# The down biases' sums in the ninth expert pair, samples' totals in four parts, ring slots at multiples of 512 bytes

## The reference, cut to what matters

```
hx = layer_norm(DN_ALPHA * x_all + o_cat @ w_out, ln1_g, ln1_b)
logits = hx @ w_router + b_router
top_val, top_idx = lax.top_k(logits, 4)                  # of 32 experts
comb = sum(one_hot(top_idx, 32) * softmax(top_val))      # 288 x 32, four non-zero a row
for e in range(32):
    gu = hx @ w_gate_up[e] + b_gate_up[e]                # 1024 x 2048
    act = clipped SwiGLU(gu)
    f += comb[:, e] * (act @ w_down[e] + b_down[e])      # 1024 x 1024
y = layer_norm(DN_ALPHA * hx + f, ln2_g, ln2_b)
```

## Time and profile before

| | |
|---|---|
| median of 3 runs | 1166.18 us (1163.85 to 1167.03) |
| the profiled execution's own time | 1164.79 us |
| its span | 1162.8 us |
| TensorE (PE) matmuls busy | 1105.6 us, 95% (5478 matmuls, 5479 weight loads) |
| VectorE (DVE) / ScalarE (ACT) / GpSimd (POOL) busy | 293.7 / 203.9 / 30.0 us |
| moved by DMA | 454.23 MB, mean 391 GB/s |
| granted TensorE clock | 0.995 of full speed |

### The profile page before, as it was taken

The page is one execution under the profiler, slowest core; times in us unless marked ns, Lnnn a source line. Parts: engine busy times, 40 slices in busy tenths (PEclk is TensorE's granted clock), DMA queues, the critical chain, the costliest instruction groups (busy, mean ns, idle before and its releaser), DMA issues.

```text
span 1162.8 us, 14168 instructions
## 1 busy us (share of the span) xinstructions
PE 1105.6 (95%) x5478; PEld 467.7 (40%) x5479; DVE 293.7 (25%) x734; ACT 203.9 (18%) x481; POOL 30.0 (3%) x65
## 2 busy tenths in 40 slices
PE   7999998999999999999999999999999999999996
PEld 5876764433333333333333333333333333333331
DVE  1453756720303021212121212020202030303123
ACT  1332422411111110202020101010101011111111
POOL 0110111000000000000000000000000000000001
PEclk9999999999999999999999999999999999999998
DMA  9958879799999999999999999999999999999992
GB/s 341 348 184 274 284 259 388 293 380 422 424 429 427 428 428 427 429 427 429 427 429 428 429 427 429 428 429 428 430 427 430 427 430 427 430 428 425 405 411 79
DMA packets 62843, 454.23 MB, mean 391 GB/s; under 512 B 6563, under 2 KB 19507, under 8 KB 35540
## 3 DMA queue, kind: packets, MB, share of 16 engines
q1 hardware_dynamic: 60322, 440.97, 91.7%
q0 software_dynamic: 1728, 10.75, 2.5%
q10 hardware_dynamic: 754, 1.98, 0.5%
HBM read 450.14 MB, written 11.93 MB: 397 GB/s over the span
## 4 chain that ended last, share of the span: by engine, by line
PE 69%; DMA 25%; DVE 2%; ACT 2%; SPq 2%; issue 1%
DMA ring<-in_w_gate_up 24%; PE bank L1167 18%; PE bank L1118 18%; PE bank L676 5%; PE bank L995 5%; PE bank L699 5%; PE bank L1272 2%; PE bank L702 2%; PE bank L860 2%; PE bank L1194 2%; PE bank L991 1%; PE bank L1302 1%; PE bank L817 1%; ACT xtok L1382 1%; ACT actT L1382 1%
## 5 line engine op out<-in xcount | busy, mean ns | idle before, releaser
L1118 PE MATMUL bank<-ring,xg 128*64 128x512 f32 x1904 | 419.3, 594 | 25.7 <-DMA ring<-in_w_gate_up 25.7
L1118 PEld LDWEIGHTS bank<-ring,xg 128*64 128x64 f32 x1904 | 141.3, 137 | 295.3 <-issue 295.2
L1167 PE MATMUL bank<-ring,actT 128*64 128x512 f32 x960 | 216.1, 597 | 3.9 <-ACT actT L1382 3.9
L2038 DVE TENSOR_TENSOR acc<-acc,bank 128x512 f32<-128x512 f32 x60 | 41.3, 688 | 496.8 <-PE bank L1194 496.7
L1532 ACT ACTIVATE sig<-gate 128x256 f32<-128x256 f32 x64 | 26.7, 417 | 541.8 <-DVE gate L2020 541.8
L1167 PEld LDWEIGHTS bank<-ring,actT 128*64 128x64 f32 x960 | 66.7, 137 | 120.3 <-issue 114.5
L2020 DVE TENSOR_SCALAR gate<-bank 128x256 f32<-128x256 f32 x64 | 26.8, 419 | 196.7 <-PE bank L1118 177.8
L699 PE MATMUL bank<-xT,wblk 128*128 128x288 f32 x256 | 67.1, 417 | 2.1 <-DMA wblk<-in_w_in 2.1
L1522 ACT ACTIVATE xg<-bank,small 128x128 f32<-128x128 f32 x128 | 48.0, 457 | 96.7 <-PE bank L676 96.7
L995 PE MATMUL bank<-hx,pick 128*128 128x512 f32 x128 | 59.2, 605 | 0.0
L1194 PE MATMUL bank<-ybuf,spread 128*128 128x512 f32 x120 | 58.4, 618 | 0.0
(11 more groups left out here) (256 smaller groups left out, 728.3 us busy)
## 6 DMA issues: line engine op xcount, KB each, us to landing
ring<-in_w_gate_up SPq DMA_DIRECT2D x119, 2048.0 KB, 25.2
ring<-in_w_down SPq DMA_DIRECT2D x63, 2048.0 KB, 26.8
ring<-in_w_gate_up SPq DMA_DIRECT2D x16, 1024.0 KB, 19.2
wblk<-in_w_in SPq DMA_DIRECT2D x12, 1024.0 KB, 8.3
kring<-in_cache_k_moba SPq DMA_DIRECT2D x16, 256.0 KB, 5.8
vring<-in_cache_v_moba SPq DMA_DIRECT2D x16, 256.0 KB, 5.6
out<-in_state_k_win POOLq DMA_DIRECT2D x8, 512.0 KB, 4.3
out<-in_state_v_win POOLq DMA_DIRECT2D x8, 512.0 KB, 5.6
```

What stands on the lines that cost most here:

```text
L1118: ins = nc.tensor.matmul(bank[n][64 * e:64 * e + 64, :], xg[:, k, 64 * e:64 * e + 64], w[e][:, 512 * n:512 * n + 512], start=False, stop=( ...
L1167: ins = nc.tensor.matmul(bank[4 + half][64 * e:64 * e + 64, :], actT[:, j, 64 * e:64 * e + 64], w[e][:, at:at + 512], start=(j == 0), stop ...
L2038: V.tensor_tensor(o, o, new, ALU.add).then_inc(S.added, 1)
```

## The change

The three parts are these. First, the work with the down biases moves from pair 14 to pair 8 on TensorE, ScalarE and VectorE; for this the loops over pairs 2 to 13 are cut in two, with pairs 8 and 9 written out between them on TensorE (pair 8 on the other two). Second, VectorE writes the samples' part, ALPHA * gain * hx, straight into `acc_s` in four instructions of 32 x 256, where it wrote `samp_x` in two of 32 x 512 and zero to `acc_s`; TensorE's four products with `ident`, VectorE's second addition and the tile `samp_x` go. Third, the ring begins at a multiple of 512 bytes (87552, up from 87168). `first` keeps its address: both expressions give 62464.

```
-    first = place("first", [128, 4096], at=cursor[0] - 16384)
+    first = place("first", [128, 4096], at=share_at + 4096)
...
+    cursor[0] += -cursor[0] % 512
     ring_at = cursor[0]
...
-    samp_x = place("samp_x", [NS, D])
...
+    MIDDLE = PAIRS // 2
...
         def add_sample_biases():
-            pe.wait_ge(S.sums_scaled, 2)
-            pe.wait_ge(S.bias_added, 2)
+            pe.wait_ge(S.bias_added, 1)
             for q in range(4):
                 r, c = slice(NS * q, NS * q + NS), slice(256 * q, 256 * q + 256)
-                nc.tensor.matmul(bank[0][r, 0:256], ident[0:NS, 0:NS], samp_x[:, c], start=True, stop=True,
-                                 tile_position=(0, NS * q))
-            for q in range(4):
-                r, c = slice(NS * q, NS * q + NS), slice(256 * q, 256 * q + 256)
-                ins = nc.tensor.matmul(bank[1][r, 0:256], combT[:, SEQ:T], bdn[:, c], start=True, stop=True,
+                ins = nc.tensor.matmul(bank[0][r, 0:256], combT[:, SEQ:T], bdn[:, c], start=True, stop=True,
                                        tile_position=(64, NS * q))
...
-        def finish_with_biases(i, m, odd):
+        def finish_with_biases(i, m, odd, m_next):
...
+            pe.wait_ge(S.bias_added, 5)
+            gate_up(i + 1, m_next, 1 - odd, {3: lambda: combine(i)}, True)
...
-        with pe.Fori(1, PAIRS // 2 - 1) as m:
+        with pe.Fori(1, MIDDLE // 2) as m:
+            finish(m * 2, m, 0, m)
+            finish(m * 2 + 1, m, 1, m + 1)
+        finish_with_biases(MIDDLE, MIDDLE // 2, 0, MIDDLE // 2)
+        finish(MIDDLE + 1, MIDDLE // 2, 1, MIDDLE // 2 + 1)
+        with pe.Fori(MIDDLE // 2 + 1, PAIRS // 2 - 1) as m:
             finish(m * 2, m, 0, m)
             finish(m * 2 + 1, m, 1, m + 1)
         last = PAIRS - 1
-        finish_with_biases(last - 1, last // 2, 0)
+        finish(last - 1, last // 2, 0, None)
...
-            pe.wait_ge(S.bias_added, 5)
             begin_gate_up(last)
...
-            for half in range(2):
-                c = slice(512 * half, 512 * half + 512)
-                V.scalar_tensor_tensor(samp_x[:, c], hx[0:NS, 2, c], ALPHA, ln_g[0:NS, c], ALU.mult,
-                                       ALU.mult).then_inc(S.sums_scaled, 1)
+            for q in range(4):
+                c = slice(256 * q, 256 * q + 256)
+                ins = V.scalar_tensor_tensor(acc_s[NS * q:NS * q + NS, :], hx[0:NS, 2, c], ALPHA, ln_g[0:NS, c], ALU.mult,
+                                             ALU.mult)
+            ins.then_inc(S.added, 1)
...
-            V.memset(acc_s[:, :], 0.0).then_inc(S.added, 1)
...
-        with dve.Fori(0, PAIRS - 2) as i:
+        with dve.Fori(0, MIDDLE) as i:
+            next_pair(i)
+        next_pair(MIDDLE, with_biases=True)
+        with dve.Fori(MIDDLE + 1, PAIRS - 2) as i:
+            next_pair(i)
         weigh_slots(PAIRS - 1, PAIRS - 1)
-        dve.wait_ge(S.added, 5 * PAIRS - 5)
-        add_biases()
-        dve.wait_ge(S.bias_added, 5)
         add_mixed(PAIRS - 2)
```

More of the change, by code:

```diff
@@ L164, in build_layer @@
     ln_gs, ln_bs = place("ln_gs", [128, 256]), place("ln_bs", [128, 256])
-    late_at = cursor[0]
     parts = spread[:, 0:128]
-    samp_x = place("samp_x", [NS, D])
     bdn = hx[64:64 + E + 1, 2, :]
-    combT = place("combT", [128, T], at=late_at)[64:64 + E + 1, :]
+    combT = place("combT", [128, T])[64:64 + E + 1, :]
     wrt = place("wrt", [128, KC, E], at=share_at)
@@ L226, in build_layer @@
         y_ready mixed added y_varied y_rooted y_scaled y_centred y_gained y_normed y_done y_moments y_shared
-        sums_whole sums_scaled copies_out
+        sums_whole copies_out
         results_out dve_done dve_moe pass_added""".split()
@@ L1220, in finish @@
                              1: lambda: (pe.wait_ge(S.actT_ready, i * 2 + 2), turn_slots(i + 1, 1))}, whole)
-            gate_up(i + 1, m_next, 1 - odd, {3: lambda: combine(i)}, next_whole)
-        def finish_with_biases(i, m, odd):
+            if m_next is not None:
+                gate_up(i + 1, m_next, 1 - odd, {3: lambda: combine(i)}, next_whole)
+        def finish_with_biases(i, m, odd, m_next):
             def first_slots():
@@ L1558, in between_pairs, with between_with_biases @@
             take_down(i)
-        def take_comb():
+        def between_with_biases(i):
+            take_gathered(i + 1)
+            take_weights(i)
+            take_turned(i)
             act.wait_ge(S.comb_turned, 1)
             copy(combT[0:E, :], bank[3][0:E, 0:T]).then_inc(S.combT_ready, 1)
-        with act.Fori(0, PAIRS - 2) as i:
+            take_slots(i + 1)
+            take_down(i)
+        with act.Fori(0, MIDDLE) as i:
             between_pairs(i)
             sigmoids(i + 1)
[L1567 to L1572, removed]
+        between_with_biases(MIDDLE)
+        sigmoids(MIDDLE + 1)
+        with act.Fori(MIDDLE + 1, PAIRS - 2) as i:
+            between_pairs(i)
+            sigmoids(i + 1)
+        between_pairs(PAIRS - 2)
         sigmoids(PAIRS - 1, (0, 1))
@@ L2047, in add_biases @@
             dve.wait_ge(S.bias_sums, 5)
-            link(V.tensor_tensor(acc_s[:, :], acc_s[:, :], bank[0][:, 0:256], ALU.add))
-            V.tensor_tensor(acc_s[:, :], acc_s[:, :], bank[1][:, 0:256], ALU.add).then_inc(S.bias_added, 1)
+            V.tensor_tensor(acc_s[:, :], acc_s[:, :], bank[0][:, 0:256], ALU.add).then_inc(S.bias_added, 1)
         largest_counts()
@@ L2057, in _, with next_pair @@
         swiglu(0)
-        with dve.Fori(0, PAIRS - 2) as i:
+        def next_pair(i, with_biases=False):
             weigh_slots(i + 1, i + 1)
+            if with_biases:
+                dve.wait_ge(S.added, 5 * i + 5)
+                add_biases()
+                dve.wait_ge(S.bias_added, 5)
             add_mixed(i)
```

## The result

The changed kernel takes 1152.88 us (median of 4 runs, 1152.73 to 1154.59), the kernel before 1166.61 beside it. The ratio is 0.989, 95% interval 0.9872 to 0.9909. By these ratios it is 11 to 13 us less than before. The prediction said 1162.0 and 1156.5 to 1165.5, so it was wrong: the gain is about three times the one forecast. The profiled execution took 1153.02, its span 1151.2.

The account below looks back on a forecast made before the run. Bound by TensorE's pace, then the weights' stream, then from 1057.70 TensorE's tail. -5.46 + 1.35 + 0 + 0 + 0.5 + 0 = -3.6 us gave 1161.2 or 1162.6; it said 1162.0, range 1156.5 to 1165.5.

Parts of the forecast that it names:

- Ring at multiples of 512: Placing the weight ring at such a multiple was taken to gain 0; bounds 18.6 us gained and 2 us lost.
- the fixed 10.2 ns a piece: DMA time per piece whatever its size, from a line through 16 KB and 4 KB pieces; 18.6 us over 1824 pieces.
- the first rival: The ring's place counts: half the fixed piece cost saved gives 1152.7 us, a quarter 1157.3; chance 0.14.
- Its rival's 1155: Time in us if the ring's place counts, worked by the Trainium skill's 256 B descriptor rule; that rival's chance 0.14.
- The biases leave the tail: Pair 14's down stretch shrinks from 22.06 to 16.60 us, so the last pair begins 5.46 us sooner.
- How much arrives: In the last pair TensorE waits 1.35 us for unit 8's weights, so 4.1 of 5.46 us arrive.
- Two more pieces of code: Cut loops fetch 9 to 10 more instruction packets in pairs 8 to 11; cost 0.5 us, bounds 0 and 6.5.
- They arrive in pair 8: The biases' work adds 4.8 us in pair 8, hidden by later waits for weights; cost 0.
- the cover: TensorE's 2.6 us of waiting for weights per pair, said to absorb pair 8's added 4.8 us after two pairs.
- Samples' totals: Four smaller VectorE writes cost 0 to 1.3 us more, hidden by 4.2 us slack before SyncE's next weights; cost 0.
- The slower rival: Fetched code holds up the weight stream in pairs 8 to 11, 6.5 us against 4.1 won: 1168; chance 0.09.
- The drowned saving: The last units' weights land later, unit 8 or 11 late by 3 us: gain 0 to 2, 1164.5; chance 0.15.

Follow-up runs that it names:

- e1: The kernel before with only the ring's begin moved, to 87552; 1159.12 us, ratio 0.9951.
- e4: The changed kernel with the ring 256 bytes higher, on a multiple of 256 but not of 512; 1154.70 us, ratio 0.9909.
- e2: The changed kernel with the ring's begin put back at 87168, so all of the change but the place; 1162.07 us, ratio 0.9971.
- e3: The changed kernel with the ring 128 bytes higher, at 87680; 1162.02 us, ratio 0.9967.
- e9: The changed kernel measured again, no edit; 1154.87 us, ratio 0.9908.
- e13: The changed kernel measured once more, no edit, on the same chip as e11 and e12; 1154.53 us, ratio 0.9897.
- e11: The changed kernel with its loops still cut but the biases' work left in pair 14; 1159.41 us, ratio 0.9936.
- e12: The changed kernel with the biases' work in pair 1 in place of pair 8, TensorE's loop over pairs 2 to 13 whole again; 1154.29 us, ratio 0.9896.
- e5: The changed kernel with the ring 32 bytes above a multiple of 512; 1163.73 us, ratio 0.9990.
- e6: The changed kernel with the ring 224 bytes above a multiple of 512; 1164.01 us, ratio 0.9981.
- e7: e2's kernel with gate, up and down products, except the last pair's, reading bias_rows and not the ring; 1162.29 us, ratio 0.997.
- e10: The changed kernel with every tile, small ones too, begun at a multiple of 256 bytes; 1154.66 us, ratio 0.9909.

## Why the prediction was wrong, step by step

*The step that failed* is "Ring at multiples of 512": "I take 0". It is worth 5.7 us by e1's ratio (3.8 to 7.7), 6.7 by its medians, and 6.0 between pair 0's first product and TensorE's last wait in the traces. Of the fixed 10.2 ns a piece that the prediction drew from its line, the misplaced start is 4.0 ns; 1824 pieces at that are 7.3 us. This is the first rival, between its quarter and its half, and it had a chance of 0.14. The sign that the prediction had named for it, 430 GB/s or more in the steady windows, came. Its rival's 1155, by the rule of the Trainium skill (DMA: Bandwidth & Descriptors, How a descriptor splits into AXI transactions), was nearer than its own sum of 1162.0. By that estimate the place would cost 0.8% of a 16 KB piece; 4.0 ns of 612 are 0.66%.

The reading behind it was at fault, not only the choice. The window of `first` (8 KB pieces, well placed) had 428 GB/s, and I set against it "steady ring units make 428 too, misplaced as they are". Its own comparison of like pieces, 420 against 428 in the earlier trace rows, it put aside as too short. The steady units are pieces of 16 KB. Their like are the ring's 8 KB pieces at 250 to 295 us, misplaced, with 422 in the trace of before; well placed they have 427 or 428 in after, e1 and e4. Both 428 and 422 could be read before the change ran, and 6 in 428 on 306 ns is 4 ns a piece, which would have given the result. A difference of 1 in 100 was called too small to see, though the argument knew that the stream bounds 600 us and multiplies it.

*The biases leave the tail*: right, 5.46 us. From the last wait to the end the tail is 4.9 us shorter in the changed kernel (105.1 to 100.2), where 4.1 was forecast.

*How much arrives*: the mechanism was right, unit 8 is the unit that is waited for where there is a wait, but its size was off: 0.39 us in the changed kernel, 0.24 in e2, 0.42 in e3 and none in e4, e9 and e13, for 1.35. In e2, whose stream is that of before, TensorE began unit 7 at 1121.71, 2.15 later than forecast (0.75 of start, 1.4 of code), and unit 8 landed at 1125.6, 1.3 later than the 1124.3 that was held fixed.

*Two more pieces of code*: right that it costs and passes to the end, but its size was off, 1.4 us for 0.5, and the price was looked for in the wrong place. The window's rate did not fall (431 in e11); one unit landed late instead (e11). The packets were 8 for "9 to 10"; 0.17 us each is an average and no price of one. With unit 8 the two errors nearly cancel: 5.46 less 1.45 and 0.24 is 3.8, the forecast 3.6, e2 3.4 (2.1 to 4.5). The agreement of the sum is better than that of its terms.

*They arrive in pair 8*: right, cost 0 by e11 against the changed kernel. The waits for the ring vanish in pair 9 and are back in pair 11, as forecast. That the cover is what makes it so, e12 speaks for from the other side: in pair 1, without cover, the same work cost 1.1 to 1.2 us by pair 7.

*Samples' totals*: right, cost 0; the four products with `ident` that go are inside the 5.46.

*The slower rival* (6.5 us of code) needed 0.43 us a packet; it was 0.17 on average. *The drowned saving* did not come: the landings of units 8 to 11 moved 7.5 to 8.0 us sooner with the stream, and unit 8 was late by 0.39.

Do the parts add up? By medians they fall short: 6.7 and 3.7 us (e1, e2) are 10.4, and the whole measured 13.7, 11.0 and 12.4. The traces, cut at pair 0's first product and at TensorE's last wait for gate and up weights, say where the rest is:

| kernel | pair 0 begins | to the last wait's end | from there to the end |
|---|---|---|---|
| before | 227.02 | 830.68 | 105.1 |
| e1: place | 225.29 | 824.66 | 105.1 |
| e2: work | 227.77 | 832.13 | 100.1 |
| after | 224.91 | 826.05 | 100.2 |
| e9: the same | 227.09 | 826.02 | 100.2 |
| e13: the same | 226.69 | 826.15 | 99.8 |

In the middle the place brings 6.0 us without the work and 6.1 with it, and the cut loops cost 1.4 or 1.5; the tail is 5 us shorter with the work and not with the place. From pair 0 on the parts add up to about 0.1 us, 9.5 to 9.8 in all. What is left is the start of pair 0, which scatters by 2 us from kernel to kernel; only about 1 us of it goes with the place.

## What to carry to other kernels

Where a DMA stream is the bound, put the tiles that it writes at multiples of 256 bytes: it costs a few bytes and gave 0.5% here (0.3 to 0.7 by e1's ratio). To judge an effect of a few ns a piece, compare pieces of the same size, over long windows or from one wait for the stream to the same wait some pairs on, and multiply by their number before calling it small. Work taken out of a tail arrives as far as the next unit of weights allows, and code that is unrolled for it is fetched on the same DMA engines: count its packets, and look for late units rather than for a lower rate.

## What the runs showed of the hardware that I had not expected

A piece written to SBUF at an address that is not a multiple of 256 bytes takes 4 to 5 ns longer: 4.0 ns when it is off by 128 bytes, 5.1 when off by 32 or 224 (16 KB pieces, e3, e5, e6); with pieces of 4 and 8 KB the difference at 128 is the same to about 1 ns.

Eight more packets of 16 KB of instructions, 0.13 MB, cost 1.4 us, where their share of the 454 MB is 0.3 us of the span. Nearly all of it came at one wait in pair 12, behind a unit that took 29.3 us to land instead of 27.9 (e11).

Behind that wait of 2.0 to 2.4 us TensorE's granted clock fell for 3.4 us to the lower of its two levels, 1.2 GHz of 2.4, in seven of the eleven traces with cut loops (after, e4, e6, e7, e9, e10, e11): the 32 products after it took 8.78 us instead of 7.09. In the changed kernel the 10 us window around them has a granted clock of 0.83:

```profile
935.00:945.00 10.00, 10.00 (x36) 3.54 (x33) 4.32 (x13) 1.25 (x3) 0.00 (x0) 0.83 1.02 436
```

In the other four (e2, e3, e5, e13), with waits of 2.00 to 2.31, it did not fall, so the wait's length alone does not decide it. Pair 13's waits took the loss up, and the end did not move: 409.90 from pair 7 to pair 14 with it, 409.88 without (e13).
